# Another order of turns, sums and scores in two attentions, and a router stage with transposes and wider blocks

## The reference

```python
# block 1
h = x @ w_in                                      # ua va za q k v zb ga gb, 1024 columns each
va = layer_norm(gelu(va));  sa = per_chunk(ws, va)
ya = gelu(ua) * sa * silu(za)
a = softmax(q0 k0) - lam * softmax(q1 k1)         # 8 heads, two causal score matrices each
yb = rms_norm(a @ v) * silu(zb)
merged = sigmoid(ga) * (ya @ w_branch_a) + sigmoid(gb) * (yb @ w_branch_b)
x = layer_norm(alpha * x + merged @ w_out + sigmoid(x @ w_ple_gate) * (p @ w_ple))
# block 2
h = rms_norm(x) * (1 + scale_m) + shift_m
o_fox = softmax(q k / 8 + decay) @ v              # 8 heads of 64
o_mla = softmax(q k / sqrt(96)) @ v               # 8 heads of 64, latent projections
x = x + gate_m * ((sigmoid(ga) * (o_mla @ wo) + sigmoid(gb) * (o_fox @ wo2)) @ w_out)
h = rms_norm(x) * (1 + scale_f) + shift_f         # called h3 in the kernel
s = sigmoid(h @ w_router)                         # 64 experts, the best 4 of 8 groups, the best 6
gate = s[chosen] / sum(s[chosen]) * 2.5
y = sum(gate_e * expert_e(h)) + (silu(h @ w_sh_gate) * (h @ w_sh_up)) @ w_sh_down
out = rms_norm(x + gate_f * y)
```

## Time and profile before

| | |
|---|---|
| median of 3 runs | 1116.52 us (1115.83 to 1118.21) |
| profiled execution | 1116.18 us, its span 1114.5 us |
| PE busy | 1060.0 us, 95% of the span |
| DVE / ACT / POOL busy | 50% / 35% / 35% |
| mean granted clock of PE | 0.978 of 2.4 GHz |
| DMA moved | 320.65 MB, 288 GB/s in the mean |

### The profile page before, as it was taken

The page is one execution under the profiler, slowest core; times in us unless marked ns, Lnnn a source line. Parts: engine busy times, 40 slices in busy tenths (PEclk is TensorE's granted clock), DMA queues, the critical chain, the costliest instruction groups (busy, mean ns, idle before and its releaser), DMA issues. The chain is left out here.

```text
span 1114.5 us, 12957 instructions
## 1 busy us (share of the span) xinstructions
PE 1060.0 (95%) x5046; PEld 705.6 (63%) x5046; DVE 560.6 (50%) x986; ACT 392.7 (35%) x677; POOL 385.3 (35%) x309
## 2 busy tenths in 40 slices
PE   8999999899999799799999999999999999999993
PEld 7788887788788687687888445444545454444442
DVE  5999768857956776655664222222222222212214
ACT  5646755546334644457333111111111111111112
POOL 1499999699940594197000000000000000000000
PEclk9999999999999899899998999999999999999998
DMA  9766665666755486254259599999999999999991
GB/s 323 249 234 216 209 203 176 241 210 217 269 185 180 152 287 209 76 190 151 90 209 390 197 392 410 419 418 417 416 416 418 418 417 416 416 417 417 418 383 39
DMA packets 88189, 320.65 MB, mean 288 GB/s; under 512 B 6688, under 2 KB 7728, under 8 KB 71232
## 3 DMA queue, kind: packets, MB, share of 16 engines
q1 hardware_dynamic: 80176, 290.90, 67.8%
q0 software_dynamic: 7664, 28.39, 7.7%
q10 hardware_dynamic: 288, 0.52, 0.1%
HBM read 318.74 MB, written 1.05 MB: 287 GB/s over the span
## 5 line engine op out<-in xcount | busy, mean ns | idle before, releaser
L810 PE MATMUL ps<-hl,L 128*128 128x512 f32 (+1 forms) x1216 | 386.4, 399 | 10.4 <-DVE rlo L1625 5.4
L810 PEld LDWEIGHTS ps<-hl,L 128*128 128x128 f32 x1216 | 229.3, 192 | 61.5 <-issue 10.9
L1625 DVE TENSOR_TENSOR rlo<-ring,hl 128x1024 fp32r<-128x1024 f32 (+1 forms) x154 | 217.3, 1434 | 83.7 <-ACT hl L1251 82.9
L810 PE MATMUL ps<-rlo,L 128*128 128x512 f32 (+1 forms) x608 | 239.5, 394 | 0.0
L810 PE MATMUL ps<-slots_all,xe 128*64 128x512 f32 (+1 forms) x1056 | 226.9, 582 | 0.8 <-DVE rt L2416 0.8
L1251 ACT ACTIVATE hl<-ring 128x1024 fp32r<-128x1024 f32 (+1 forms) x154 | 159.4, 1055 | 159.4 <-PE ps L810 107.0
L799 POOL CAST two<-ident 64x128 fp32r<-64x128 f32 x64 | 18.9, 295 | 506.3 <-PE ps L810 504.8
L752 POOL TENSOR_SCALAR mring<-mring,st 128x512 f32<-128x512 f32 x84 | 178.6, 2126 | 1.6
L810 PEld LDWEIGHTS ps<-slots_all,xe 128*64 128x64 f32 x1056 | 73.9, 137 | 131.7 <-issue 128.5
L810 PEld LDWEIGHTS ps<-rlo,L 128*128 128x128 f32 x608 | 116.2, 191 | 24.6
L754 POOL TENSOR_TENSOR macc<-macc,mring 128x512 f32<-128x512 f32 x84 | 121.6, 1448 | 7.0
(11 more groups left out here) (213 smaller groups left out, 951.9 us busy)
## 6 DMA issues: line engine op xcount, KB each, us to landing
slots_all<-in_w_exp_gate SPq DMA_DIRECT2D x64, 1024.0 KB, 19.6
slots_all<-in_w_exp_up SPq DMA_DIRECT2D x64, 1024.0 KB, 15.6
slots_all<-in_w_exp_down SPq DMA_DIRECT2D x64, 1024.0 KB, 16.4
ring<-in_w_in SPq DMA_DIRECT2D x48, 1024.0 KB, 5.5
mring<-in_w_mod POOLq DMA_DIRECT2D x48, 512.0 KB, 4.3
ring<-in_w_out SPq DMA_DIRECT2D x8, 1024.0 KB, 5.1
ring<-in_w_ple_gate SPq DMA_DIRECT2D x4, 1024.0 KB, 6.1
ring<-in_w_branch_a SPq DMA_DIRECT2D x4, 1024.0 KB, 5.6
```

The source lines that it names most:

```text
L810: return e.matmul(o, l, r, start=start, stop=stop)
L1625: return e.tensor_tensor(o, a, b, op)
```

## The change

Three things are changed.

1. **Order in the attentions.** On PE, `head` and `pair` now do the turns, then the weighted sums, then the scores. On ACT the copy of turned weights stays at step 1, and the exponentials are made at step 2, one piece later; at a block's end they follow the copy. On DVE the copy of `o` comes first, then the maxima, at step 1; the normalisation moves to step 3, behind two more roundings. For pairs, the copy of turned weights and the division go ahead of the maxima. The banks are named in the new order.
2. **Order of two loads.** The two loads of `zb0` come ahead of `aln`.
3. **Router stage.** DVE scales the rows, `xp` = x / rms, 128 × 1024 at once, and PE turns `xp` by transposes, one instruction for each block. Router and the first 192 gate columns of the shared expert are one product of 256 columns from one slot (`shared`); the other 64 gate columns and the 256 up columns are one of 320 from a place of their own (`shb`), loaded by SP behind the ring's last load once the latent keys are turned. `h3` is turned back in two parts between the router products. The normalisation of the gates on DVE moves behind the gather matrix, and the turns of ranks, gates and shared part on PE move behind the first gather, which now takes banks 4 to 7. `loads2` has one entry instead of three at its head, so two more expert loads stand in its first round of 15.

The core of the diff, first the loads and PE's router stage:

```diff
-        for name in ("q0 q1 k0 k1 v0 v1 za0 za1 ua0 ua1 va0 va1 aln zb0 ws zb1 gb0 gb1 ga0 ga1 "
+        for name in ("q0 q1 k0 k1 v0 v1 za0 za1 ua0 ua1 va0 va1 zb0 aln ws zb1 gb0 gb1 ga0 ga1 "
...
-        load2("router", 8, pk(D["w_router_2"], 8))
-        load2("sg", 8, pk(D["w_sh_gate_2"], 8))
-        load2("su", 8, pk(D["w_sh_up_2"], 8))
+        WR, WSG, WSU = (pk(D[q], 8) for q in ("w_router_2", "w_sh_gate_2", "w_sh_up_2"))
+        load2("shared", 8, WSG[:, :, 0:192])
...
+            w.wait_ge(pe_aux.sem, pe_aux.at[("km", 1, 4)])
+            e.dma_start(shb[:, :, 0:64], WSG[:, :, 192:256]).then_inc(shared_in, 16)
+            e.dma_start(shb[:, :, 64:320], WSU).then_inc(shared_in, 16)
...
             h3_turn(0)
...
-            route(br, 0)
+            route(br, 0, (4, 5, 6, 7))
             h3_turn(1)
-            b0 = take(("sh", 0))
-            shared_half(b0, 0, "sg", wsg, 0)
-            taken(route(br, 1))
-            taken(shared_half(b0, 0, "su", wsu, 256))
-            turn("h3", lambda m, j: ht3[:, j, tok(m)], lambda m, j0: None)
+            route(br, 0, (0, 1, 2, 3))
+            h3_back(0)
+            taken(route(br, 1, (4, 5, 6, 7, 0, 1, 2, 3)))
+            h3_back(1)
+            taken(shared_rest(take(("sh", 0)), 0, range(8)))
```

On ACT:

```diff
             square2(1, 0)
+            h3_shift(0)
             square2(1, 1)
...
-                    if n == 1 and four:
-                        between(name, 0)
+                    if n == 1 and four:
+                        for h in HEADS_IN.get(name, ()):
+                            weights_of_head(h)
...
+                    if n == 2 and four:
+                        for h in HEADS_IN.get(name, ()):
+                            probs_of_head(h)
```

On DVE:

```diff
+                    if n == 1 and four:
+                        for h in HEADS_IN.get(name, ()):
+                            maxes_of_head(h)
...
+                    if n == 3 and four:
+                        for h in HEADS_IN.get(name, ()):
+                            probs_of_head(h)
...
-            def diagonal2(m):
+            def scaled_rows(m):
...
-                tsc(DIAG2(m), ident[:, :], st[:, 70 + m:71 + m], None, ALU.mult, None).then_inc(xp_set, 1)
+                tsc(xp[:, m, :], R[:, m, :], st[:, 70 + m:71 + m], None, ALU.mult, None).then_inc(xp_set, 1)
```

More of the change, by code:

```diff
@@ L969, in pair @@
                                      for u in range(2)], 64)
+                if s < 4:
+                    wait_turned("qm" if n0 else "qf")
+                    wait_turned("km" if n0 else "kf")
+                    scores([("s2", n, u) for u in range(2)], lambda u: QM[0:width, 2 * s + u, :],
+                           lambda u: KMT[0:width, 2 * s + u, :], n)
             def x_ready(m, kk):
@@ L1078, in _ @@
             project("wp0", L0, l_ready("mT2"), {1: lambda: merged_turn2(1)})
-            wr = slot2("router")[:, 0:512].rearrange("p (k n) -> p k n", k=8)
-            wsg, wsu = (slot2(n).rearrange("p (k n) -> p k n", k=8) for n in ("sg", "su"))
+            wrg = slot2("shared").rearrange("p (k n) -> p k n", k=8)
             wsd = slot2("sd").rearrange("p (k n) -> p k n", k=2)
@@ L1189, in shared_down @@
                 wait_turned("h3")
-                wait_read(("sT", 0), ("sT", 1), *aux_names[aux_dense - 4:aux_dense], *(("mod", c) for c in MOD_SUM["end"]))
+                wait_read("router", ("sT", 0), ("sT", 1), *(("g", 0, k) for k in range(4, 8)), *aux_names[aux_dense - 4:aux_dense], *(("mod", c) for c in MOD_SUM["end"]))
                 w.wait_ge(*here2("sd"))
@@ L1316, in probs, with weights_of_head @@
                 x.then_inc(aux_a.sem, 1)
[L1318 to L1321 removed]
+            def weights_of_head(s):
                 if 1 <= s < 9:
@@ L1366, in project @@
                     keep(name, dst, f, pre)
-                between(name, 1 if four else 0)
+                for n0, q in pairs_in(name, 1 if four else 0):
+                    weights_of_pair(n0, q)
+                    probs_of_pair(n0, q)
             def turned(name, dst, width=128, pre=None, groups=(0, 4)):
@@ L1543, in _, with h3_high @@
             project("wp0", at={2: second_turned, 3: lambda: square2(0, 0)})
+            def h3_high(m):
+                for j0 in (0, 4):
+                    aux_done(("h3", m, j0))
+                    act(h3hl[:, 0, m, 128 * j0:128 * j0 + 512], bank(("h3", m, j0))[:, :], ACT.Copy).then_inc(th.sem, 1)
             square2(0, 1)
@@ L1797, in maxes, with maxes_of_head, probs_of_head @@
                     x.then_inc(maxed, 1)
-            def head(s):
+            def maxes_of_head(s):
+                if s >= 2:
+                    h = s - 2
+                    aux_done(("o", h))
+                    e.tensor_copy(OO[:, :, 128 * h:128 * h + 128],
+                                  bank(("o", h))[:, 0:256].rearrange("p (m d) -> p m d", m=2)).then_inc(aux_v.sem, 1)
+                if s < 8:
+                    maxes([("s", s, u) for u in range(2)], stats_at(s), 1.0)
+            def probs_of_head(s):
                 if s < 8:
                     st0 = stats_at(s)
-                    maxes([("s", s, u) for u in range(2)], st0, 1.0)
                     w.wait_ge(*read(("s", s, 1)))
@@ L2294, in _ @@
             h3_shift(1)
-            w.wait_ge(*read("router"))
+            h3_low(0)
+            w.wait_ge(sc_set, 1)
             mine(tt(CH, SC, brd[:, 384:448].unsqueeze(1).to_broadcast([128, 2, 64]), ALU.add))
@@ L2428, in _ @@
             gathered(0)
+            w.wait_ge(th_g, 1)
+            tt(rgt[64:128, 1, :], bank("gT")[64:128, 0:256], rgt[64:128, 1, :].bitcast(F32), ALU.subtract)\
+                .then_inc(aux_v.sem, 1)
             turned_p(0)
```

227 lines of the change are left out of this document (112 added, 115 removed).

## The result

The changed kernel took 1099.77 us in the median of four executions (1098.05 to 1102.30), the kernel before 1116.17 (1111.48 to 1118.21). The ratio is 0.9861, with a 95% interval from 0.9822 to 0.9899. The profiled execution of the changed kernel took 1102.30 us, its span is 1100.6, 13.9 less than before.

The account below looks back on a forecast made before the run. PE was taken as the bound, its chain and the transfers hanging on the first gate and up matmuls at 623.97 us. Gains of 1.0 + 7.8 + 4.8 = 13.6 us gave 1102.5 us, range 1095 to 1112.

Parts of the forecast that it names:

- The rival of the transfers: Experts' stretch: the expert loads become the bound, 61 us for four pairs against PE's 59.08; 1106 us, chance 0.05.
- Part 1: First attention, new order and exchanged loads: a gain of 1 us, bounds −2 and 3.6.
- the 0.89 stays: First attention: PE's 0.89 us wait for the rounding behind the layer norm remains, as the layer norm isn't moved on DVE.
- the clock term: First attention: the new gap of about 4.0 us at head 5 costs one half-clock stretch, 2 us.
- the other heads at nothing: First attention: the turns of the other seven heads cost nothing, with about 1.5 us of cover on DVE.
- the wait of 1.65: First attention: PE's 1.65 us wait for rounded weights at 189.26 goes, because exchanging the two loads issues zb1's weights earlier.
- Part 2: Second attention, sums ahead of scores: PE's waits for exponentials go, a gain of 7.8 us, bounds 4 and 10.5.
- The costly place: Second attention, 453.90 to 465.69 us: the 5.18 us bank wait can't arise, sums end at 460.45, a gain of 5.1.
- Part 3: Router stage: 42.38 us becomes 35.3, a gain of 7.1, less 2.3 for the clock: 4.8 net, bounds 1.5 and 8.3.
- the two gaps should bring the same fall: Router stage: PE gaps of 1.75 and 0.7 us bring a half-clock stretch costing about 3.5 us, against 1.2 before.
- The first rival: Router stage: the clock stays low because turns don't hold it, so the stage gives −1.7 us; 1109 us, chance 0.13.
- The slower rival: First attention: DVE's normalisation reaches PE late in every head, 2 us at each of eight; 1119.6 us, chance 0.10.

Follow-up runs that it names:

- the run of this part alone: The kernel before with only the first attention's new order and the new order of the two loads: 1117.42 us, ratio 1.0031.
- the square: Changed kernel, first attention's order by load order: old/old 0.9842, old/new 0.9833, new/old 0.9805, new/new 0.9861 and 0.9863 of the kernel before.
- order1_undone: The changed kernel with the first attention's old order put back and the new order of the two loads kept: 1093.06 us, ratio 0.9833.
- gap_wider: The changed kernel with two unread copies on ACT lengthening PE's gap behind the router stage's first turn: 1101.88 us, ratio 0.9887.
- att2_only: The kernel before with the second attention's new order alone: 1105.97 us, ratio 0.9916.
- router_only: The kernel before with the new router stage alone: 1102.77 us, ratio 0.9891.
- norm5_early: The changed kernel with head 5's exponentials and normalisation put back to step 1, ahead of the two roundings: 1093.01 us, ratio 0.9808.

## Why the prediction was right, and where not

The sum came out: 13.6 us were forecast, 13.9 is the difference of the profiled executions and 16.4 that of the medians. Two of the three terms were wrong, and their errors, 4.9 and 5.3 us, cancelled: that the sum came out is luck. What was right is the bound of the kernel and the mechanism of the second attention.

1. **What bounds the kernel** held. PE's chain and the transfers hang on the first gate and up products; 13.93 us there are 13.9 at the end, and 59.08 did not change. PE waits once between 620 and 1075 us, 0.83 us, as it did before. The rival of the transfers is refuted.
2. **Part 1 had the wrong sign:** +1 forecast, −3.9 in the trace, −3.4 in the run of this part alone (−1.3 to −5.5); the stated bound was −2. The mechanism was named, and the end of the normalisation, 188.2, came at 188.60. Two steps failed. PE was free at 183.37, not at 184.15, since the 0.89 ahead of it went as well (the step "the 0.89 stays": the layer norm ran 1.65 us earlier), so the wait was 5.38 instead of 4.0. And the clock term was sized too small: 13.65 us at half clock with 10.88 of work, some 5.4 lost, against the 2 that I put down for one stretch. A third term, the other heads at nothing, held in the main: the wait of 1.66 us near 227 went with the one at head 5. What the prediction did not see is whose doing the two roundings were. It counted the exchange of the loads as a gain of 1.65 and the roundings as part of the new order; the square shows that the exchange is what put them there. In the old order the exchange does lift the wait of 1.65 (order1_undone).
3. **Part 2** had the right mechanism: exponentials at 460.44, or 456.35 on the time scale of before, against 456.55; a wait of 2.50 against 2.65. The total of 8.0 us against 7.8 is better than its two terms. The costly place gave 4.0 instead of 5.1, since turns, sums and scores took 5.1 us, mostly at half clock, where 3.9 at full clock were forecast. Behind it 4.1 us came instead of 2.7: 2.8 of idle time, and the same work in 69.8 us of PE's busy time instead of 71.1.
4. **Part 3 was mis-sized in two terms:** 10.15 instead of 4.8, above the bound of 8.3. At full clock the forecast was 35.3 us and the stage took 32.23. The turns were priced at 0.24 each, the price of the diagonal's products with the same strided weights; a transpose takes 0.13, 1.05 for eight, so 1.7 us were too much. The wait for the scaled rows was 0.25 instead of 0.7; the scaling itself took 0.75 us, as estimated. The 320-column price held as busy time (5.01 for nine, 0.556 each), but groups overlap at their ends: from start to start the sixteen took 8.4 us instead of 9.0. The rest are small terms, among them 0.1 in the sum that no step names. The other term is the clock, 2.3 net: the step "the two gaps should bring the same fall" failed. Before, the gap was 2.11 us, now it is 1.69, and the clock stayed up.
5. **The first rival is refuted** in this stage: four groups of turns lay between the products and the clock was 1.00 throughout. The Trainium skill, TensorE: Matmul & The Clock Gate, Part 4 (PE-mode transpose), speaks of transposes as not counting for the clock gate; no run of this stage shows a loss by it, neither the changed kernel nor the one with products in their place; the one fall, in gap_wider, came with a longer gap. The stretch of the earlier trace rows from which I argued for it is no support: block 1 of att2_only and of router_only is that of before, and in their profiles no half-clock stretch comes there.
6. **The slower rival** named the right mechanism and the right cause for its limit: it took one head, not all, and that head stands at the layer norm. The run with all heads put back gave nothing more.

What stays open: in the second attention DVE's maxima, late behind rotations, set the last wait of 2.50 us and with it, in eight profiles of eleven, a half-clock stretch of 6.83 us; this wasn't tried. Nor is it shown why DVE's operations take longer in one kernel than in another.

## What to carry to other kernels

A step that is moved later in an engine's program is moved past whatever a plan puts between, and an edit elsewhere, here the order of two loads, can change that plan: list the rows of that engine for each edit alone and for both. An idle gap of PE should be priced with the half-clock stretch that may follow it, which can cost as much as the gap. A buffer that is held longer delays the load that goes into it, and with that whatever stands behind the load in another engine's program. And when a sum of several terms comes out, look at the terms: two of three were wrong here, and the best kernels were found at the one that had the wrong sign.

## What the hardware showed that was not expected

- A transpose of a 128 × 128 fp32 block whose weights are read with a stride takes 0.13 us behind another; an fp32 product of the same block and stride is two instructions of 0.24 (1.05 against 3.85 us for eight blocks).
- The length of a gap alone does not give the length of the half-clock stretch that goes with it. A gap of PE of 5.4 us in the first attention went with 13.65 us at half clock, begun inside the gap, in each of five profiles; the gap of 5.18 us in the second attention, with the old order, with 6.83 us in each of three. One of 2.50 us there, with the new order, went with 6.83 us in eight profiles and with none in three. One of 1.86 us was followed by 3.41 us or by none in the same code, one of 1.69 by none in ten profiles, one of 1.67 at another place by 3.41.
- DVE's normalisation of head 5 took 2.6 us before (183.47 to 186.07), 2.8 in norm5_early (182.13 to 184.91), 3.5 with the old loads (183.46 to 186.98) and 4.4 after (184.19 to 188.60) with the same instructions; why is not shown. A sum of DVE times in this stretch can be off by as much. Its first row before:

```profile
183.47 0.18 DVE L1806 RECIPROCAL st<-st 128x4 f32<-128x4 f32 x1 [1.25 <-ACT ex L1251]
```
